# Memory keys and values as one 512-column product, a bfloat16 mask product and transposed token factors in a kernel of two transformer blocks

## Chip, cores and metric

The kernel runs on one core of a Trainium2 chip. The metric is the device time of one execution in microseconds (us), the median of several runs.

## The reference, cut to what matters

Two transformer blocks run one after the other over 256 tokens of width 1024. The first has two layers (a gated linear recurrence, HGRN2, then a latent attention, MLA), each with an attention to a memory of 256 tokens beside it and a convolutional feed-forward layer behind it. The second has a feed-forward layer, a mixer of a convolution and gated linear attention, another feed-forward layer and a gated output. All of it is float32. What the change touches:

```python
def memory_attention(qm, mem_n, w_mem_kv, qn_g, kn_g):
    kv = mem_n @ w_mem_kv                       # (256, 1024) @ (1024, 512)
    q = rms_norm(qm.reshape(B, S, MEM_HEADS, MEM_HDIM), qn_g)
    k = rms_norm(kv[..., :MEM_W].reshape(B, M, MEM_HEADS, MEM_HDIM), kn_g)
    v = kv[..., MEM_W:].reshape(B, M, MEM_HEADS, MEM_HDIM)
    s = jnp.einsum('bshd,bmhd->bhsm', q, k) * (MEM_HDIM ** -0.5)
    p = jax.nn.softmax(s, axis=-1)
    ...
# causal_block_attention (MLA, 6 heads)
    s = jnp.where(kpos[None, :] <= qpos[:, None], s, -jnp.inf)
# in front of every feed-forward layer and of the second block's mixer
    y = xf * lax.rsqrt(jnp.mean(xf * xf, axis=-1, keepdims=True) + EPS)
# in the convolution module of the second block: a LayerNorm, with one factor for each token
```

## The kernel before, in words

**Weights as a stream.** All large weights lie in one DRAM tensor `stream` of units, 128 partitions x 3072 floats (1.5 MB) each. SyncE loads unit u into slot u % 3 of `raw`; its order and its waits are written by hand (lines 343 to 387): unit u is asked for as soon as VectorE has split unit u - 3. ScalarE rounds each third (a "piece", 1024 columns) of a unit to float32r (`w_hi`, helper `copy`, line 1162; `split`, line 1180), VectorE subtracts it from the raw weight (`w_lo`, line 1743). Each engine's program is one fixed list, so a wait holds up all that stands behind it on that engine.

**Products.** A float32 product is made of three float32r matmuls (`three`, lines 418 to 420): high x high, high x low and low x high parts. `rows` (line 425) makes one with the tokens as stationary operand and the weight's columns moving, for 2 token tiles and 8 contraction tiles, so 48 matmuls; `cols` makes one with the weight as stationary operand and 256 tokens moving. `full` (line 423) is a plain matmul of any type; on float32 operands the profile records two matmuls for each.

**The start.** TensorE works through six units in this order (lines 727 to 761): the forget gates U_F and U_F + 1 (and, between them, the transposed memory), the memory's keys and values of layer 0, U_MEM0 and U_MEM0 + 1, and the queries U_Q and U_Q + 1. U_MEM0 holds 384 of the 512 columns, made in PSUM banks 0 and 1; U_MEM0 + 1 holds the other 128, made in banks 2 and 3. ScalarE evacuates a unit's banks right behind the product (`unit`, line 1184), and from the third unit on TensorE waits for the evacuation of the unit two back. For the memory product the normed memory must be there as high and low part (`y_hi` by ScalarE, `y_lo` by VectorE, line 1999, semaphore `memT_lo_done`). VectorE then norms the keys (`mem_keys`, line 1923).

**The recurrence.** Eight levels of small matmuls on float32 (`level`) alternate with rows-products: U_I, U_I + 1, U_MEM1 (384 of layer 1's memory columns, banks 4 and 5), U_MEM1 + 1 (the other 128, and 256 columns of layer 0's memory queries, banks 6 and 7), then U_G into banks 4 and 5 and U_G + 1.

**The causal mask** is added to the scores of MLA by a matmul of identity x mask, both float32, 256 columns wide, as the first of each head's accumulation (`head_S`, line 901). Around it TensorE transposes the head's queries and keys (`head_T`, line 898), ScalarE copies them, VectorE takes the maxima (line 2280), ScalarE the exponentials, VectorE scales them (lines 2289 to 2292), TensorE transposes them (`head_P`, line 924), VectorE copies that (line 2298), and `head_O` multiplies with the values. VectorE's list is: maxima of head 0, the key group 2 (from line 2258, it waits for ScalarE's query sums), maxima of head 1, scaling of head 0, maxima of head 2, copy of head 0, and so on.

**The tokens' factors.** A norm's factor for each token stands as a column [128 tokens, 1]; `spread` (line 527) makes it a row that is the same on all partitions: matmul with the column broadcast to 128x128 as stationary operand and the identity moving, twice, for four feed-forward layers and the second mixer; a sixth such place is in the LayerNorm (behind U_OUT2's fourth contraction tile).

Of the kernel before, what the change touches and what calls it, by code (L numbers as in the profile page):

```python
# [133 lines left out]
def build(nc, stream, vectors, masks, x_in, mem_in, pos_in, ple_in, fin_in, out):  # L134
    with ExitStack() as ctx:
# [193 lines left out]
        PLAIN = [0, 1, 2, 3, 4, 5] + HG_UNITS + [U_MLA, U_MLA + 1, U_MLA + 2, U_UQ, U_UQ + 1, U_UKV] + \  # L329
# [13 lines left out]
        def _(sp):  # L343
            i0 = _cols["ident"][0]
            for t in range(T):
# [12 lines left out]
            sp.dma_start(raw[:, 2, :], stream[2]).then_inc(rings[2], 16)  # L358
# [31 lines left out]
        def _(pool):  # L390
            pool.memset(zero[:, :], 0.0).then_inc(sem("zero_set"), 1)

            pool.wait_ge(sem("memT_lo_done"), 2)
            pool.memset(A(4608, HEADS * S), 0.0).then_inc(sem("r_zero"), 1)
# [9 lines left out]
            m.then_inc(sem("gA_clear"), 1)  # L404
# [7 lines left out]
        def _(pe):  # L412
# [310 lines left out]
            pe.wait_ge(sem("zero_set"), 1)  # L723
# [4 lines left out]
            for n, u in enumerate((U_F, U_F + 1, U_MEM0, U_MEM0 + 1, U_Q, U_Q + 1)):  # L728
                if n >= 2:
                    pe.wait_ge(s_evac, EV[u - 2])  # L730
                if u == U_MEM0:
                    pe.wait_ge(sem("memT_lo_done"), 1)
                    m = rows(u, 0, 384, (0, 1), y_hi, y_lo)
                elif u == U_MEM0 + 1:
                    m = rows(u, 0, P, (2, 3), y_hi, y_lo)
# [1937 lines left out]
```

## Time and profile before

| | us |
|---|---|
| median of 3 runs | 1179.88 |
| lowest and highest run | 1179.79 and 1180.44 |
| span of the profiled execution | 1179.2 |
| TensorE busy in it | 1167.9 (99%) |
| VectorE busy | 934.7 (79%) |
| ScalarE busy | 730.9 (62%) |

The profiled execution's own device time isn't listed apart from its span; the span is 0.7 us under the median. In the timelines below a row gives the start of a group in us from the span's start, then its length, then engine, line, operation, operands and count. A matmul's length contains its latency, and matmuls overlap: what one costs TensorE is the distance from its start to the next one's start. In brackets stands the idle time before it and what ended that.

### The profile page before, as it was taken

Reading aid. Unit: us, or ns where it says so; the run is one execution under the profiler, and the core shown is the slowest. Engines: PE = TensorE matmul, PEld = TensorE weight load, DVE = VectorE, ACT = ScalarE, POOL = GpSimd, SP = SyncE. Lnnn points to the kernel's source line nnn. Section 1 sums busy time; section 2 is a strip of 40 time slices with the busy share of each in tenths; the row PEclk is TensorE's granted clock in tenths of the full one; section 3 lists DMA queues with packets and bytes.
Section 4 is the critical chain, followed back from the end, with each engine's and each line's share of the span. In section 5 each row is a group of like instructions: output and inputs, shape, how many; then the busy total and the mean of one; then the engine's idle time right before and its main releaser. Section 6 shows DMA issues by size and latency. Waiting matters only on the chain.

```text
span 1179.2 us, 19449 instructions
## 1 busy us (share of the span) xinstructions
PE 1167.9 (99%) x7030; PEld 1038.7 (88%) x7030; DVE 934.7 (79%) x1831; ACT 730.9 (62%) x1353; POOL 4.1 (0%) x11
## 2 busy tenths in 40 slices
PE   9999999999999999999999999999999999999997
PEld 7999979888899888988889988888999898888886
DVE  6988878998878878998887866665799777666666
ACT  5883657666656876766665655544667665555555
POOL 0000000000000000000000000000000000000000
PEclk9999999999999999999999999999999999999999
DMA  8545253545455514555555564545454146454540
GB/s 333 215 155 190 80 197 136 216 184 208 165 215 176 199 55 161 214 215 178 195 183 198 208 214 172 202 176 198 161 184 192 49 158 249 168 205 171 203 161 36
DMA packets 21316, 211.64 MB, mean 179 GB/s; under 512 B 2625, under 2 KB 2881, under 8 KB 4481
## 3 DMA queue, kind: packets, MB, share of 16 engines
q1 hardware_dynamic: 20880, 208.90, 48.6%
q0 software_dynamic: 368, 1.84, 0.5%
q8 instruction: 43, 0.70, 0.2%
q14 instruction: 25, 0.20, 0.0%
HBM read 209.68 MB, written 1.05 MB: 179 GB/s over the span
## 4 chain that ended last, share of the span: by engine, by line
PE 93%; DVE 4%; ACT 2%; DMA 1%; issue 1%; SPq 0%; DVEq 0%; ACTq 0%
PE ps L423 39%; PE ps L418 18%; PE ps L419 17%; PE ps L420 17%; PE ps L523 1%; DVE w_lo L1743 1%; DMA x<-in_x 1%; PE ps L898 0%; ACT w_hi L1162 0%; ACT arena L1162 0%; PE ps L698 0%; DVE arena L2145 0%; DVE h_both L1825 0%; ACT L1719 0%; ACT L1652 0%
## 5 line engine op out<-in xcount | busy, mean ns | idle before, releaser
L1743 DVE TENSOR_TENSOR w_lo<-raw,w_hi 128x1024 fp32r<-128x1024 f32 (+1 forms) x390 | 448.2, 1166 | 25.7 <-ACT w_hi L1162 25.6
L1162 ACT ACTIVATE w_hi<-raw 128x1024 fp32r<-128x1024 f32 (+1 forms) x390 | 383.4, 1010 | 30.2 <-PE ps L420 26.0
L423 PE MATMUL ps<-h_both,w_hi 128*128 128x512 f32 x1088 | 386.9, 398 | 0.0
L423 PE MATMUL ps<-h_both,w_lo 128*128 128x256 f32 x1088 | 305.7, 281 | 0.0
L423 PEld LDWEIGHTS ps<-h_both,w_hi 128*128 128x128 f32 x1088 | 204.8, 188 | 49.7
L418 PE MATMUL ps<-w_hi,y_hi 128*128 128x512 f32 (+2 forms) x550 | 211.7, 385 | 0.9 <-DVE y_lo L2195 0.8
L419 PE MATMUL ps<-w_lo,y_hi 128*128 128x512 f32 (+2 forms) x550 | 208.9, 380 | 0.0
L420 PE MATMUL ps<-w_hi,y_lo 128*128 128x512 f32 (+2 forms) x550 | 208.1, 378 | 0.0
L423 PEld LDWEIGHTS ps<-h_both,w_lo 128*128 128x128 f32 x1088 | 205.7, 189 | 2.6
L1162 ACT ACTIVATE arena<-ps 128x256 f32<-128x256 f32 (+2 forms) x166 | 57.7, 396 | 151.8 <-PE ps L423 148.3
L418 PE MATMUL ps<-h_both,w_hi 128*128 128x256 f32 x520 | 148.6, 286 | 0.0
L419 PE MATMUL ps<-h_both,w_hi 128*128 128x256 f32 x520 | 147.3, 283 | 0.0
L420 PE MATMUL ps<-h_both,w_lo 128*128 128x256 f32 x520 | 147.3, 283 | 0.0
L1846 DVE TENSOR_TENSOR arena<-ps,arena 128x256 f32<-128x256 f32 x136 | 51.3, 419 | 101.6 <-ACT arena L1162 101.6
L418 PEld LDWEIGHTS ps<-w_hi,y_hi 128*128 128x128 f32 x550 | 103.5, 188 | 21.6 <-issue 2.0
L420 PEld LDWEIGHTS ps<-w_hi,y_lo 128*128 128x128 f32 x550 | 103.5, 188 | 19.2
L419 PEld LDWEIGHTS ps<-w_lo,y_hi 128*128 128x128 f32 x550 | 103.6, 188 | 14.6
L419 PEld LDWEIGHTS ps<-h_both,w_hi 128*128 128x128 f32 x520 | 99.8, 192 | 0.5
L418 PEld LDWEIGHTS ps<-h_both,w_hi 128*128 128x128 f32 x520 | 99.8, 192 | 0.5
L420 PEld LDWEIGHTS ps<-h_both,w_lo 128*128 128x128 f32 x520 | 99.8, 192 | 0.0
L1262 ACT ACTIVATE arena<-arena,vec 128x256 f32<-128x256 f32 x88 | 48.2, 595 | 79.1 <-DVE arena L1851 44.3
L1868 DVE SCALAR_TENSOR_TENSOR arena<-arena,vec 128x254 f32<-128x254 f32 (+1 forms) x176 | 77.2, 480 | 22.6 <-ACT arena L1262 22.3
(288 smaller groups left out, 1319.9 us busy)
## 6 DMA issues: line engine op xcount, KB each, us to landing
raw<-in_stream SPq DMA_DIRECT2D x129, 1536.0 KB, 6.6
raw<-in_stream SPq DMA_DIRECT2D x3, 512.0 KB, 8.3
x<-in_x SPq DMA_DIRECT2D x2, 512.0 KB, 5.4
arena<-in_mem SPq DMA_DIRECT2D x1, 1024.0 KB, 14.1
x<-in_x POOLq DMA_DIRECT2D x1, 1024.0 KB, 5.1
out<-arena SPq DMA_DIRECT2D x4, 256.0 KB, 2.1
vec<-in_vectors SPq DMA_DIRECT2D x1, 633.0 KB, 8.4
arena<-in_final POOLq DMA_DIRECT2D x1, 512.0 KB, 4.8
```

The source lines that it names most:

```text
L418: pe.matmul(o, lh, rh, start=start, stop=False, skip_group_check=True)
L419: pe.matmul(o, lh, rl, start=False, stop=False, skip_group_check=True)
L420: return pe.matmul(o, ll, rh, start=False, stop=stop, skip_group_check=True)
L423: return pe.matmul(o, l, r, start=start, stop=stop, skip_group_check=True)
L523: m = pe.transpose(xt(i, k)[:, t * P:(t + 1) * P], x[:, t, k * P:(k + 1) * P], ident)
L1162: return act.activation(o, i, ACT.Copy, scale=scale)
L1262: act.activation(cv[:, g, z * S:(z + 1) * S], tu[:, g, z * S:(z + 1) * S], ACT.Identity, scale=w(4 * z + 2), bias=w(4 * z + 3)).then_inc(s ...
L1743: dve.tensor_tensor(w_lo[:, s, a], raw[:, s, a], w_hi[:, s, a], ALU.subtract).then_inc(s_lo, 1)
L1846: dve.tensor_tensor(tu[:, g, z * S:(z + 1) * S], ps[:, half_bank(j, z), 0:S], second(i)[:, g, z * S:(z + 1) * S], ALU.add).then_inc(sem("h ...
L1868: m = dve.scalar_tensor_tensor(c, tu[:, g, z * S:(z + 1) * S - d], w, c, ALU.mult, ALU.add)
```

## The change

Three parts. (1) The 512 columns of a layer's memory product are made in two banks by one product: the load of U_MEM0 (and of U_MEM1) now gathers contraction tiles 0 to 5 with all 512 columns from two units of the same DRAM tensor, in two DMAs, one of 384-column runs (1536 B) and one of 128-column runs (512 B); the next unit gathers tiles 6 and 7. U_MEM0 + 1 has one piece to split instead of three. In layer 1 the memory queries' 256 columns fill the rest of U_MEM1 + 1, with a third DMA. The evacuation of layer 0 comes after both units, that of layer 1 too; the queries change banks. SyncE's loads of the first 12 units are written out instead of partly looped. (2) GpSimd copies identity and mask to bfloat16 once, and the mask product uses those. (3) The six spreads are PE transposes. GpSimd's semaphores become one counter.

```diff
+MEM_UNITS = {U_MEM0: 1, U_MEM0 + 1: 1, U_MEM1: 1, U_MEM1 + 1: 2}
-        used = {U_UQ: 3 * 768, R_UQ1: 3 * 384, ...
+        used = {U_MEM0 + 1: PIECE, U_UQ: 3 * 768, R_UQ1: 3 * 384, ...
...
+        Q_BANK, OWN_BANK = {1: 2, 4: 2, 5: 0}, (2, 3, 0)
-        PLAIN = [0, 1, 2, 3, 4, 5] + HG_UNITS + ...
+        PLAIN = [0, 1, 3, 4, 5] + HG_UNITS + ...
...
+            def memory_unit(u):
+                v = U_MEM0 if u < U_MEM1 else U_MEM1
+                ks = slice(0, 6) if u == v else slice(6, KT)
+                n, ring = 2 * MEM_W * (ks.stop - ks.start), rings[u % SLOTS]
+                to = raw[:, u % SLOTS, 0:n].rearrange("p (k n) -> p k n", n=2 * MEM_W)
+                a, b = (stream[v + i].rearrange("p (k n) -> p k n", n=NC3) for i in range(2))
+                sp.dma_start(to[:, :, 0:NC3], a[:, ks, :]).then_inc(ring, 16)
+                sp.dma_start(to[:, :, NC3:2 * MEM_W], b[:, ks, 0:P]).then_inc(ring, 16)
+                if u == U_MEM1 + 1:
+                    to = raw[:, u % SLOTS, n:UNIT].rearrange("p (k n) -> p k n", n=MEM_W)
+                    sp.dma_start(to, b[:, :, P:NC3]).then_inc(ring, 16)
...
-            sp.dma_start(raw[:, 2, :], stream[2]).then_inc(rings[2], 16)
+            memory_unit(U_MEM0)
...
-            at = 1
+            for u in range(SLOTS, U_OUT0):
+                one(u)
+            at = U_OUT0 // SLOTS
...
+            pool.wait_ge(sem("ident_loaded"), 16)
+            pool.wait_ge(sem("vec_loaded"), 16 * 2)
+            pool.tensor_copy(mask_b[:, 0, :], ident)
+            pool.tensor_copy(mask_b[:, 1, :], causal).then_inc(sem("pool_done"), 1)
...
+            def mem_rows(l, part, banks):
+                u = (U_MEM0, U_MEM1)[l] + part
+                for k in ((0, 1, 2, 3, 4, 5), (6, 7))[part]:
+                    a = (k - 6 * part) * 2 * MEM_W
+                    pe.wait_ge(s_lo, pieces(u, a + 2 * MEM_W))
+                    for t in range(T):
+                        tt, r = slice(t * P, (t + 1) * P), slice(a, a + 2 * MEM_W)
+                        m = three(ps[:, banks[t], :], y_hi[:, k, tt], y_lo[:, k, tt],
+                                  w_hi[:, u % SLOTS, r], w_lo[:, u % SLOTS, r], k == 0, k == KT - 1)
+                return m
...
-                    m = full(ps[:, 7, t * P:(t + 1) * P], NORM[:, t:t + 1].to_broadcast([P, P]), ident)
+                    m = pe.transpose(ps[:, 7, t * P:(t + 1) * P], NORM[:, t:t + 1].to_broadcast([P, P]), ident)
...
-                if n >= 2:
-                    pe.wait_ge(s_evac, EV[u - 2])
                 if u == U_MEM0:
+                    pe.wait_ge(s_evac, EV[U_F])
                     pe.wait_ge(sem("memT_lo_done"), 1)
-                    m = rows(u, 0, 384, (0, 1), y_hi, y_lo)
+                    m = mem_rows(0, 0, (0, 1))
                 elif u == U_MEM0 + 1:
-                    m = rows(u, 0, P, (2, 3), y_hi, y_lo)
+                    m = mem_rows(0, 1, (0, 1))
...
                 else:
+                    if n >= 2:
+                        pe.wait_ge(s_evac, EV[(U_F + 1, U_MEM0 + 1)[u - U_Q]])
...
-                    m = rows(u, 0, 384, b, y_hi, y_lo)
+                    m = mem_rows(1, 0, (4, 5))
                 else:
-                    rows(u, 0, P, b, y_hi, y_lo)
-                    m = rows(u, P, MEM_W, b, h_hi, h_lo, col=P)
+                    mem_rows(1, 1, (4, 5))
+                    m = rows(u, PIECE, MEM_W, b, h_hi, h_lo, width=MEM_W)
...
-                full(bank[:, 0:2 * P].rearrange("p (a b) -> p a b", b=P), ident,
-                     causal.unsqueeze(1).to_broadcast([P, 2, P]), True, False)
+                if h == 0:
+                    pe.wait_ge(sem("pool_done"), 3)
+                full(bank[:, 0:2 * P].rearrange("p (a b) -> p a b", b=P), mask_b[:, 0, :],
+                     mask_b[:, 1, :].unsqueeze(1).to_broadcast([P, 2, P]), True, False)
...
-            unit(U_MEM0, *[lambda t=t: copy(mk_tok[0][:, t, :], ps[:, t, 0:256]) for t in range(T)],
-                 *[lambda t=t: copy(mem_v[:, 0, t, 0:P], ps[:, t, 256:384]) for t in range(T)])
+            split(U_MEM0 + 2)
+            def memory(l, banks):
+                act.wait_ge(s_used, (U_MEM0, U_MEM1)[l] + 2)
+                for t in range(T):
+                    copy(mk_tok[l][:, t, :], ps[:, banks[t], 0:MEM_W])
+                for t in range(T):
+                    m = copy(mem_v[:, l, t, :], ps[:, banks[t], MEM_W:2 * MEM_W])
+                evac.inc(m)
...
-            unit(U_MEM0 + 1, *[lambda t=t: copy(mem_v[:, 0, t, P:256], ps[:, 2 + t, 0:P]) for t in range(T)])
+            split(U_MEM0 + 3)
+            memory(0, (0, 1))
...
                 elif u == U_MEM1:
-                    unit(u, *tok(mk_tok[1], b, 256), *tok(mem_v[:, 1], b, P, 0, 256))
+                    split(u + 2)
                 elif u == U_MEM1 + 1:
-                    unit(u, *tok(mem_v[:, 1], b, P, P), *tok(qm0, b, MEM_W, 0, P))
+                    split(u + 2)
+                    memory(1, (4, 5))
+                    evac_only(u, *tok(qm0, b, MEM_W))
...
-                dve.wait_ge(s_evac, EV[(U_MEM0, U_MEM1)[l]])
+                dve.wait_ge(s_evac, EV[(U_MEM0 + 1, U_MEM1)[l]])
```

## Rows read from the trace of the kernel before

**Rows 1.** The page, part 1: busy us, share of the span, instructions.

```profile
PE 1167.9 (99%) x7030; PEld 1038.7 (88%) x7030; DVE 934.7 (79%) x1831; ACT 730.9 (62%) x1353; POOL 4.1 (0%) x11
```

**Rows 2.** TensorE's longest wait of six: us in total, times, longest.

```profile
PE ps L423 <- POOL zero L391: 1.0, 1, 1.0
```

**Rows 3.** Timeline of TensorE: layer 0's memory product, and what follows.

```profile
36.74 0.34 PE L418 MATMUL ps<-w_hi,y_hi 128*128 128x384 f32 x1
...
45.07 0.22 PE L418 MATMUL ps<-w_hi,y_hi 128*128 128x128 f32 x1
...
50.38 0.33 PE L418 MATMUL ps<-h_both,w_hi 128*128 128x256 f32 x1
```

**Rows 4.** Timeline of TensorE: layer 1's memory product, with a level between.

```profile
95.41 0.42 PE L418 MATMUL ps<-w_hi,y_hi 128*128 128x384 f32 x1
...
103.81 0.33 PE L423 MATMUL ps<-arena 128*128 128x64 f32 x2
...
106.41 0.31 PE L418 MATMUL ps<-w_hi,y_hi 128*128 128x128 f32 x1
...
111.80 0.34 PE L418 MATMUL ps<-w_hi,h_both 128*128 128x256 f32 x1
```

**Rows 5.** Timeline of TensorE: 36 matmuls of 512 columns, then 16 transposes.

```profile
155.34 0.50 PE L418 MATMUL ps<-w_hi,y_hi 128*128 128x512 f32 x1
...
163.64 0.27 PE L698 MATMUL ps<-vec,arena 128*128 128x128 f32 x1
...
165.30 0.48 PE L418 MATMUL ps<-w_hi,y_hi 128*128 128x512 f32 x1
```

**Rows 6.** Timeline of TensorE: a spread (two products, four records) and what follows.

```profile
186.41 0.69 PE L423 MATMUL ps<-vec,small 128*128 128x128 f32 x4
186.86 0.36 PE L418 MATMUL ps<-h_both,w_hi 128*128 128x256 f32 x1
```

**Rows 7.** Timeline of TensorE in MLA: head 0's mask and P, head 1's O.

```profile
411.49 0.60 PE L423 MATMUL ps<-vec 128*128 128x256 f32 x2
411.93 1.69 PE L423 MATMUL ps<-arena 128*128 128x128 f32 x12
...
419.71 0.52 PE L924 MATMUL ps<-vec,arena 128*128 128x128 f32 x3
...
424.79 0.92 PE L423 MATMUL ps<-mem_v,arena 128*128 128x256 f32 x4
```

**Rows 8.** Timeline of VectorE: key group 2, head 0's scaling, head 1's copy.

```profile
414.68 0.36 DVE L2258 TENSOR_SCALAR small<-small 128x2 f32<-128x2 f32 x2
...
419.21 0.35 DVE L2292 TENSOR_SCALAR arena<-arena,small 128x256 f32<-128x256 f32 x1
...
424.18 0.55 DVE L2298 COPY mem_v<-ps 128x384 f32<-128x384 f32 x1
```

**Rows 9.** Line 358, the load of U_MEM0, issued at 8.0 us.

```profile
DMA to landing us min/median/max: 16.8/16.8/16.8
```

**Rows 10.** Windows: us, busy (instructions) by engine, clock, DMA share, GB/s.

```profile
24.00:26.00 2.00, 2.00 (x19) 1.89 (x18) 1.96 (x5) 2.00 (x4) 0.00 (x0) 1.00 1.06 448
163.60:165.30 1.70, 1.70 (x17) 1.66 (x16) 1.43 (x9) 0.00 (x0) 0.00 (x0) 1.00 0.00 0
```

**Rows 11.** DMA issues by size, KB each, median us to landing.

```profile
vec<-in_vectors SPq DMA_DIRECT2D x1, 64.0 KB, 3.9
```

**Rows 12.** Timeline of ScalarE: splits of U_F + 1 and of U_MEM0.

```profile
22.10 5.77 ACT L1162 ACTIVATE w_hi<-raw 128x1024 fp32r<-128x1024 f32 x6
```

**Rows 13.** Timeline of VectorE: memory's low part, splits of units 3 and 4.

```profile
32.44 3.27 DVE L1999 SCALAR_TENSOR_TENSOR y_lo<-arena,vec,y_hi 128x256 fp32r<-128x256 f32 x8
...
37.66 3.49 DVE L1743 TENSOR_TENSOR w_lo<-raw,w_hi 128x1024 fp32r<-128x1024 f32 x3
...
46.86 3.49 DVE L1743 TENSOR_TENSOR w_lo<-raw,w_hi 128x1024 fp32r<-128x1024 f32 x3
```

**Rows 14.** Timeline of ScalarE: evacuation of the memory queries, two copies.

```profile
118.13 0.67 ACT L1162 ACTIVATE x<-ps 128x256 f32<-128x256 f32 x2
```

More of the change, by code:

```diff
@@ L106, in extent @@
     else:
-        used = {U_UQ: 3 * 768, R_UQ1: 3 * 384, U_OUT0 + 2: 2 * D, U_OUT1 + 2: 2 * D, U_OUT2: 2 * D,
+        used = {U_MEM0 + 1: PIECE, U_UQ: 3 * 768, R_UQ1: 3 * 384, U_OUT0 + 2: 2 * D, U_OUT1 + 2: 2 * D, U_OUT2: 2 * D,
                 U_PROJ: 2 * D, U_GATE + 2: 2 * D}.get(u, UNIT)
@@ L159, in build @@
         zero = sb("zero", [P, P], BF16)
+        mask_b = sb("mask_b", [P, 2, P], BF16)
         trig = sb("trig", [P, 2, T, HALF])
@@ L327, in build @@
         PE_TAPS = [(3, tap) for tap in range(TAPS)] + [(2, tap) for tap in range(SHARED)]
-        PLAIN = [0, 1, 2, 3, 4, 5] + HG_UNITS + [U_MLA, U_MLA + 1, U_MLA + 2, U_UQ, U_UQ + 1, U_UKV] + \
+        PLAIN = [0, 1, 3, 4, 5] + HG_UNITS + [U_MLA, U_MLA + 1, U_MLA + 2, U_UQ, U_UQ + 1, U_UKV] + \
                 [U_IN2, U_IN2 + 1, U_IN2 + 2, U_IN2 + 3, U_IN2 + 5, U_IN2 + 6, U_PROJ]
@@ L370, in one @@
                 sp.wait_ge(s_lo, (u - SLOTS) * 3 + 3)
+                if u in MEM_UNITS:
+                    memory_unit(u)
+                    return
                 sp.dma_start(raw[:, u % SLOTS, :], stream[SWAPPED.get(u, u)]).then_inc(rings[u % SLOTS], 16)
-            at = 1
+            for u in range(SLOTS, U_OUT0):
+                one(u)
+            at = U_OUT0 // SLOTS
             for a, b in ((U_UQ // SLOTS, U_UKV // SLOTS + 1), (U_OUT2 // SLOTS, (U_OUT2 + 2) // SLOTS + 1)):
@@ L390, in _ @@
         def _(pool):
-            pool.memset(zero[:, :], 0.0).then_inc(sem("zero_set"), 1)
+            pool.memset(zero[:, :], 0.0).then_inc(sem("pool_done"), 1)
             pool.wait_ge(sem("memT_lo_done"), 2)
-            pool.memset(A(4608, HEADS * S), 0.0).then_inc(sem("r_zero"), 1)
+            pool.memset(A(4608, HEADS * S), 0.0).then_inc(sem("pool_done"), 1)
+            pool.wait_ge(sem("ident_loaded"), 16)
+            pool.wait_ge(sem("vec_loaded"), 16 * 2)
+            pool.tensor_copy(mask_b[:, 0, :], ident)
+            pool.tensor_copy(mask_b[:, 1, :], causal).then_inc(sem("pool_done"), 1)
             pool.wait_ge(sem("hg_o_ready"), T + 1)
@@ L403, in _ @@
                 m = pool.memset(gA[par][CHUNK:P, :, 0:CHUNK], 0.0)
-            m.then_inc(sem("gA_clear"), 1)
+            m.then_inc(sem("pool_done"), 1)
             pool.wait_ge(sem("late_factors"), LATE.index(6) + 1)
@@ L721, in beside_memory @@
                 pe.wait_ge(sem("y_ready"), k + 1)
-            pe.wait_ge(sem("zero_set"), 1)
+            pe.wait_ge(sem("pool_done"), 1)
             warm(34)
@@ L765, in own @@
                     n, tt = h * T + t, slice(t * P, (t + 1) * P)
-                    m = full(ps[:, n // 4, (n % 4) * P:(n % 4 + 1) * P], hk[:, h, tt], hq[:, h, tt])
+                    m = full(ps[:, OWN_BANK[n // 4], (n % 4) * P:(n % 4 + 1) * P], hk[:, h, tt], hq[:, h, tt])
                     if n % 4 == 3:
@@ L1114, in gla_y @@
                     for t in range(T):
-                        m = full(ps[:, 5, t * P:(t + 1) * P], LN[:, t:t + 1].to_broadcast([P, P]), ident)
+                        m = pe.transpose(ps[:, 5, t * P:(t + 1) * P], LN[:, t:t + 1].to_broadcast([P, P]), ident)
                     m.then_inc(sem("ln_ready"), 1)
@@ L1172, in hi @@
                 elif p == 0:
-                    n = u // SLOTS + (s > 0)
+                    n = u // SLOTS + (s > 0) + sum(e for v, e in MEM_UNITS.items() if v <= u and v % SLOTS == s)
                     act.wait_ge(rings[s], 16 * n if r is None else r * 16 + 16 * n)
@@ L1377, in queries @@
                 evac_only(U_Q + n,
-                          lambda: act.activation(hq[:, h:h + 2, :].rearrange("p a b -> p (a b)"), ps[:, 2 * n, :], ACT.Silu),
-                          lambda: act.activation(hq[:, h + 2, :], ps[:, 2 * n + 1, 0:S], ACT.Silu))
+                          lambda: act.activation(hq[:, h:h + 2, :].rearrange("p a b -> p (a b)"), ps[:, 2 - 2 * n, :], ACT.Silu),
+                          lambda: act.activation(hq[:, h + 2, :], ps[:, 3 - 2 * n, 0:S], ACT.Silu))
             split(U_Q + 2)
@@ L1393, in exps @@
                         act.wait_ge(sem("ln_done"), half + 1)
-                        act.wait_ge(sem("r_zero"), 1)
+                        act.wait_ge(sem("pool_done"), 2)
                     act.activation(right(hE[:, hh, :], m), right(hD[:, hh, :], m), ACT.Exp)
@@ L1637, in _ @@
             act.wait_ge(sem("g_s_ready"), 1)
-            act.wait_ge(sem("gA_clear"), 1)
+            act.wait_ge(sem("pool_done"), 4)
             for par in range(2):
```

4 lines of the change are left out of this document (2 added, 2 removed).

## The prediction

> **What bounds the kernel now.** I read the page's busy shares first: TensorE is busy 1167.9 us of 1179.2, VectorE 79%, ScalarE 62% [rows 1]. Then TensorE's waits: there are six, and the longest is 1.0 us [rows 2]. So nearly every microsecond is a TensorE slot, and a slot saved is time saved, as long as what TensorE asks for next is ready that much earlier. The question for each edit is thus double: how many slots go, and how early the next operand was. For slots I take the timeline, distance from one start to a later start, since a matmul's printed length overlaps the next one. For readiness I compare the end of the producer on ScalarE or VectorE with TensorE's start. All durations come from one profiled execution with a span of 1179.2 us; the median of the runs is 1179.88, and what lies around the span isn't listed, so I subtract the sum from the median and take the surroundings as unchanged. A difference of 0.2%, 2.4 us, is about what a measurement of this kernel can tell from none.
>
> **Part 1, the memory product.** Layer 0 now: 48 matmuls of 384 columns take 45.07 - 36.74 = 8.33 us (0.174 each), and 48 of 128 columns take 50.38 - 45.07 = 5.31 us (0.111 each) [rows 3]. A third of the columns costs two thirds of the time: the narrow ones are paid by the matmul, not by the column. Layer 1: 103.81 - 95.41 = 8.40 and 111.80 - 106.41 = 5.39 [rows 4]. The change makes 48 matmuls of 512 columns instead of 96. Their price stands in the trace: 36 take 163.64 - 155.34 = 8.30 us, 0.231 each with a slow first one [rows 5]; 48 come to 11.0 us. Gain in layer 0: 13.64 - 11.0 = 2.6 us; in layer 1: 13.79 - 11.0 = 2.8 us. Together **5.4 us** of slots. The memory queries' 48 matmuls keep their width.
>
> Is what follows ready? Five places:
>
> (a) The load of U_MEM0 now is 768 runs of 1536 B and 768 of 512 B, where it was 128 long rows. It landed at 8.0 + 16.8 = 24.8 us [rows 9], behind a queue that was full: DMA share 1.06, 448 GB/s [rows 10]. ScalarE began to split it at 22.10 + 3 x 0.96 = 25.0 [rows 12], so it has only 0.2 us in hand. Behind that split come ScalarE's evacuation, the memory's high part, and VectorE's low part, which ended at 32.44 + 3.27 = 35.7 [rows 13]; TensorE began the product at 36.74 [rows 3]. So a landing up to 0.2 + 1.0 = 1.2 us later costs nothing. No row shows a large load in short runs. By bytes alone nothing changes: 1.5 MB at 448 GB/s are 3.5 us either way, and earlier than that is excluded, since the bytes are the same. The upper end is the 64 KB load, 8 runs of 512 B for each of 16 engines, which took 3.9 us [rows 11], at most 0.49 us a run; but most of that is the way to the first byte and back, paid once. I take the end by bytes plus half a microsecond or so, since in a full queue nothing is paid once per run that isn't hidden behind other engines' work; that costs TensorE nothing.
>
> The Trainium skill, DMA: Bandwidth & Descriptors, section "Bandwidth" (Measured), speaks against short runs: it gives a floor of about 10.5 ns a packet. An estimate by it: 96 instead of 8 runs for each engine are 88 x 10.5 ns = 0.9 us later, within the 1.2 us in hand, so the sum would stay the same; no row here shows it.
>
> (b) TensorE reaches U_Q 2.6 us earlier, at 47.7. VectorE's list is full from the memory's low part on, so it must get shorter. It does: U_MEM0 + 1 is one piece instead of three, 3.49 us before [rows 13], two of three pieces go, 2.3 us less 0.3 for two stubs of 2 columns, so 2.0. The split of U_Q's first piece then ends at 46.86 + 1.2 - 2.0 = 46.1 [rows 13], 1.6 us ahead; its other pieces are asked for no faster than they come.
>
> (c) The evacuation of layer 0 comes later in the list, but the queries now go to banks 2 and 3, free since U_F + 1, so nobody waits for it but the key norm, and the keys' transposes stand behind the whole of U_Q.
>
> (d) In layer 1 the new wait is U_G for banks 4 and 5. In front of it TensorE has a level, 106.41 - 103.81 = 2.6 us [rows 4]. ScalarE must copy four times 256 columns, two of which take 0.67 us [rows 14]: 1.3 us and 0.2 to start, so 1.1 us in hand. Queued behind these copies are the exponentials of level 5, some 0.5 us later; VectorE's products for that level were ahead of TensorE by over 1 us, as no wait in this stretch shows.
>
> (e) SyncE's list is unrolled in the same order; two or three DMAs in place of one for U_MEM1 are issued long before they are split. GpSimd's two copies stand behind its clearing of the recurrence's tile and before the reload of x, which comes only when the recurrence is done; the mask is needed at 411.49 [rows 7].
>
> **Part 2, the mask.** A float32 mask product costs 411.93 - 411.49 = 0.44 us [rows 7]. In bfloat16 it is one matmul of 256 columns; its price lies between the 0.11 of 128 columns [rows 3] and the 0.23 of 512 [rows 5], I take 0.12. Six heads: 6 x 0.32 = 1.9 us of slots. But here readiness fails. TensorE's P of head 0 starts at 419.71 [rows 7], and VectorE's scaling that it needs ends at 419.21 + 0.35 = 419.56 [rows 8]. That comes from a VectorE list that has been full since key group 2 at 414.68 [rows 8], which waits for ScalarE's sums of a product that precedes the first mask. So the three masks before P of head 0 give back their 1.0 us there: TensorE will wait. The same for head 1's O: the copy ends at 424.18 + 0.55 = 424.73 [rows 8] and TensorE starts at 424.79 [rows 7], so the fourth mask is lost too. Behind it VectorE has idle time and follows TensorE; of the last two masks I count one and a bit. **0.4 us** of 1.9.
>
> **Part 3, the spreads.** Two float32 products are four records, 186.86 - 186.41 = 0.45 us [rows 6]. Sixteen transposes take 165.30 - 163.64 = 1.66 us [rows 5], so two take 0.2. Six spreads: 6 x 0.22 = **1.3 us**; bounds 1.0 and 1.5. What follows a spread is a product whose weights are ready, and the receivers get their factors earlier, not later.
>
> The Trainium skill, TensorE: Matmul & The Clock Gate, "Part 4: PE-mode transpose", says transposes don't count as busy for the clock. By it, trading products for transposes could only cost. Here 16 transposes in a row ran at a granted clock of 1.00 (2.4 GHz) [rows 10], after a stretch of full work; two in a row are less of a gap, so I give the rule no share in the sum.
>
> **The sum.** 5.4 + 0.4 + 1.3 = 7.1 us: 1179.88 - 7.1 = **1172.8 us**.
>
> **The rivals.**
>
> Mask whole. If VectorE's list in MLA moves up after all, all six masks count: 5.4 + 1.9 + 1.3 = 8.6, 1171.3 us. For it: the slots are there. Against: rows 7 and 8 leave 0.15 and 0.06 us. Chance 0.13.
>
> Late landing. U_MEM0 comes 2.2 to 5.2 us later, TensorE waits 1 to 4 us in front of the memory product: 1174 to 1177 us. For it: the chain of (a) has 1.2 us in hand and an unknown price. Chance 0.14.
>
> Full lists at the start. ScalarE and VectorE are so dense until 65 us that a new order costs one of them a microsecond; half of layer 0's gain goes: 1174.1. Against: both lose two pieces. Chance 0.09.
>
> Slower: run cost. The mechanism is the same queue as in (a), but priced by the run. To end slower than before by 0.2% the load must come 7.1 + 2.4 + 1.2 = 10.7 us later. With 96 runs for each engine that is (3.5 + 10.7) / 96 = 148 ns a run; from there on it decides. At 200 ns the load takes 19.2 us, 15.7 later, TensorE waits 14.5, and the time is 1187.3. Rows 11 don't exclude it (490 ns at most), but a full queue at 448 GB/s makes it unlikely. Chance 0.04.
>
> No effect. The wide product saves slots, but TensorE waits as long somewhere later, a stage being timed by something that doesn't move (a transfer, or VectorE in the recurrence): 1179 to 1180. Against: TensorE has almost no wait anywhere [rows 2], so no stage is now timed by others except the stretch in MLA. Chance 0.05.
>
> My own case has 0.55.
>
> **The numbers.** The likeliest case gives 1172.8. The range takes in the mask whole and the bounds of the wide product (10.9 to 11.1 us) below, and most of the late landing above: 1170.9 to 1175.8. Faster by over 0.2% (under 1177.5): 0.55 + 0.13 + 0.09 + 0.12 of the late landing = 0.89; within 0.2%: 0.05 + 0.02 = 0.07; slower 0.04.
>
> **What would show it.** Right: 48 matmuls of 512 columns in about 11 us twice, none of 128 with `y_hi`; the same product starting near 36.7; U_Q near 47.7 with no wait; a new wait of about 1 us of TensorE in front of P of head 0 (line 924), released by VectorE; transposes of `small`, 12 in all. Wrong: a wait of TensorE on `y_lo` of line 1999 (the landing), on ScalarE in front of U_G (the banks), or no wait at line 924 (then the mask counts whole). The whole forecast falls if 512 columns cost more than 0.28 us each there.

## The result and the profile after

The kernel after takes 1172.63 us (median of 5 runs, 1171.99 to 1173.66), the kernel before beside it 1179.88 (1179.75 to 1180.44): ratio 0.9937, 95% interval 0.9925 to 0.9949, so between 6.0 and 8.8 us faster. The forecast was 1172.8. The span of the profiled execution fell from 1179.2 to 1170.3 us, 8.9; how these two numbers go together comes below.

The page after, part 1 (busy us, share, instructions), answers to [rows 1]:

```profile
PE 1158.6 (99%) x6916; PEld 1025.4 (88%) x6916; DVE 932.4 (80%) x1831; ACT 728.5 (62%) x1349; POOL 6.4 (1%) x13
```

TensorE has 114 matmuls fewer: 96 in the memory products, 6 masks that are one record instead of two, 6 spreads with two records instead of four. It is still 99% busy, but its list of waits is no longer the one of [rows 2]. After (us in total, times, longest):

```profile
PE ps L966 <- DVE arena L2344: 1.4, 2, 1.0
PE ps L450 <- POOL zero L413: 1.0, 1, 1.0
PE ps L445 <- DVE y_lo L2247: 0.8, 1, 0.8
PE ps L903 <- DVE arena L2197: 0.7, 1, 0.7
PE ps L562 <- DVE h_both L1877: 0.5, 1, 0.5
PE ps L450 <- DVE mem_v L2350: 0.3, 1, 0.3
PE ps L450 <- ACT arena L1704: 0.3, 1, 0.3
```

L966 is `head_P`: two new waits behind VectorE's scaling. `L450 <- DVE mem_v` is new too, `head_O` behind VectorE's copy. The rest was there; of the six waits before, the 0.7 us in front of the first norm is gone.

The timeline of TensorE, layer 0's memory product (to [rows 3]), then layer 1's (to [rows 4]):

```profile
35.95 0.47 PE L445 MATMUL ps<-w_hi,y_hi 128*128 128x512 f32 x1
...
46.95 0.28 PE L445 MATMUL ps<-h_both,w_hi 128*128 128x256 f32 x1
...
91.93 0.47 PE L445 MATMUL ps<-w_hi,y_hi 128*128 128x512 f32 x1
...
100.22 2.79 PE L450 MATMUL ps<-arena 128*128 128x64 f32 x24
102.81 0.48 PE L445 MATMUL ps<-w_hi,y_hi 128*128 128x512 f32 x1
...
105.66 0.28 PE L445 MATMUL ps<-w_hi,h_both 128*128 128x256 f32 x1
```

Layer 0: 46.95 - 35.95 = 11.00 us where 13.64 stood. Layer 1's first six tiles take 100.22 - 91.93 = 8.29; then comes a level, and the last two tiles take 105.66 - 102.81 = 2.85. Together 11.14, where 13.79 stood. U_Q has no wait in front of it.

The spread of the first feed-forward layer (to [rows 6]) costs 180.39 - 180.22 = 0.17 us where it was 0.45, and the granted clock around it is 1.00 (window: us, busy and instructions by engine, clock, DMA share, GB/s):

```profile
180.22 0.41 PE L570 MATMUL ps<-vec,small 128*128 128x128 f32 x2
180.39 0.36 PE L445 MATMUL ps<-h_both,w_hi 128*128 128x256 f32 x1
```

```profile
180.20:180.60 0.40, 0.40 (x7) 0.40 (x6) 0.40 (x1) 0.05 (x1) 0.00 (x0) 1.00 0.00 0
```

MLA in TensorE's timeline (to [rows 7]): a mask product costs 405.20 - 405.09 = 0.11 us, and three places wait (in brackets):

```profile
405.09 0.27 PE L450 MATMUL ps<-mask_b 128*128 128x256 bf16 x1
405.20 1.70 PE L450 MATMUL ps<-arena 128*128 128x128 f32 x12
...
413.31 0.52 PE L966 MATMUL ps<-vec,arena 128*128 128x128 f32 x3 [0.96 <-DVE arena L2344]
...
418.12 0.92 PE L450 MATMUL ps<-mem_v,arena 128*128 128x256 f32 x4 [0.32 <-DVE mem_v L2350]
...
425.17 0.55 PE L966 MATMUL ps<-vec,arena 128*128 128x128 f32 x3 [0.40 <-DVE arena L2344]
```

They are P of head 0, O of head 1 and P of head 4. Before, TensorE stood about 0.1 us at each of the three, too short for its list of waits.

**Where the 8.9 us of the span are.** I cut TensorE's timeline at four starts: the first norm's transposes, the memory product, `head_T(0)` in MLA, and U_OUT1's product behind MLA. An ordinary table, each length a difference of two starts (the last one: span minus start):

| us | before | after | difference |
|---|---|---|---|
| span's start to norm | 12.09 | 11.19 | 0.90 |
| norm to memory product | 24.65 | 24.76 | -0.11 |
| memory product to T of head 0 | 369.59 | 363.98 | 5.61 |
| MLA, T of head 0 to U_OUT1 | 26.79 | 26.20 | 0.59 |
| U_OUT1 to the span's end | 746.08 | 744.17 | 1.91 |

Part 1 and one spread are in the third line, part 2 in the fourth, five spreads in the fifth. Two things in it are no slot of the change. The first line is when `x` and its first statistics came: over the 14 profiled executions of this study the norm started anywhere from 10.45 to 12.26 us, whatever the kernel. In these two profiles the second load of `x` landed at 8.4 us before and at 7.5 after. And 0.6 of the last line lies behind the last operation of VectorE; an experiment below is about it. From the norm on the difference is 8.00 us, without the 0.6 it is 7.4.

The second line hides a loss: `e2_mask_alone` and `e3_spreads_alone` below, which leave this stretch as it was before, took 24.48 us in it, so 24.76 is 0.28 us more and not 0.11.

The device time also has a part outside the span. Device time minus span, taken execution by execution (spans are listed to 0.1 us), was 1.74 to 1.83 us in 48 executions of the kernel before (timed beside the experiments; the medians of their spans were 1178.0 to 1178.5 us on the four chips) and 1.99 to 3.06 us, median 2.52, in the five of the kernel after (median span 1170.3). So some 0.7 us of what the span lost came back outside it, which is why the medians differ by 7.25 us only. What that part is and why it grew, no run here shows.

### The profile page after: what moved, and what is told of

Same layout as the page of the kernel before. It is cut to its first block, busy times and chain, and to the rows that moved or that the text cites. A ratio compares the mean times of both kernels' runs of the same rounds, so it can differ in the third digit from the quotient of the medians.

```text
span 1170.3 us, 19211 instructions
## 1 busy us (share of the span) xinstructions
PE 1158.6 (99%) x6916; PEld 1025.4 (88%) x6916; DVE 932.4 (80%) x1831; ACT 728.5 (62%) x1349; POOL 6.4 (1%) x13
## 4 chain that ended last, share of the span: by engine, by line
PE 94%; DVE 4%; ACT 2%; issue 0%; POOL 0%; DVEq 0%; ACTq 0%; POOLq 0%
PE ps L450 39%; PE ps L445 18%; PE ps L446 17%; PE ps L447 17%; PE ps L562 1%; DVE w_lo L1795 1%; ACT arena L1204 0%; PE ps L737 0%; DVE arena L2197 0%; ACT w_hi L1204 0%; PE ps L938 0%; DVE arena L2322 0%; DVE h_both L1877 0%; DVE small L2333 0%; PE ps L570 0%
## 5 line engine op out<-in xcount | busy, mean ns | idle before, releaser
L450 PE MATMUL ps<-h_both,w_hi 128*128 128x512 f32 x1088 | 386.8, 398 | 0.0
L450 PE MATMUL ps<-h_both,w_lo 128*128 128x256 f32 x1088 | 305.4, 281 | 0.0
L450 PEld LDWEIGHTS ps<-h_both,w_hi 128*128 128x128 f32 x1088 | 204.4, 188 | 50.0
L450 PEld LDWEIGHTS ps<-h_both,w_lo 128*128 128x128 f32 x1088 | 205.4, 189 | 2.6
L445 PE MATMUL ps<-w_hi,y_hi 128*128 128x512 f32 (+1 forms) x518 | 204.6, 395 | 1.0 <-DVE y_lo L2247 0.8
L446 PE MATMUL ps<-w_lo,y_hi 128*128 128x512 f32 (+1 forms) x518 | 201.7, 389 | 0.0
L447 PE MATMUL ps<-w_hi,y_lo 128*128 128x512 f32 (+1 forms) x518 | 201.0, 388 | 0.0
L445 PEld LDWEIGHTS ps<-w_hi,y_hi 128*128 128x128 f32 x518 | 97.3, 188 | 23.2 <-issue 2.2
L447 PEld LDWEIGHTS ps<-w_hi,y_lo 128*128 128x128 f32 x518 | 97.3, 188 | 20.5
L446 PEld LDWEIGHTS ps<-w_lo,y_hi 128*128 128x128 f32 x518 | 97.4, 188 | 15.8
```

The lines of the kernel that those rows point to most:

```text
L445: pe.matmul(o, lh, rh, start=start, stop=False, skip_group_check=True)
L446: pe.matmul(o, lh, rl, start=False, stop=False, skip_group_check=True)
L447: return pe.matmul(o, ll, rh, start=False, stop=stop, skip_group_check=True)
L450: return pe.matmul(o, l, r, start=start, stop=stop, skip_group_check=True)
```

## The experiments

Each was timed in 5 rounds against the kernel before on the same chip (5 executions; 11 of e2 and e3, 4 of e11). The start of an execution scatters by about 1 us, and so do single executions of one kernel. For changes under 1 us I therefore read the lengths of the table above. Where nothing in them was changed, MLA repeats to 0.1 us and the stretch before it to 0.2 us (363.81 to 364.00 in after, e5, e6, e7, e9 and e12).

**The parts one by one.** `e1_memory_alone` is the kernel after with float32 mask and spreads, without GpSimd's copies:

```diff
-  full(bank[:, 0:2 * P].rearrange(...), mask_b[:, 0, :], mask_b[:, 1, :].unsqueeze(1).to_broadcast([P, 2, P]), True, False)
+  full(bank[:, 0:2 * P].rearrange(...), ident, causal.unsqueeze(1).to_broadcast([P, 2, P]), True, False)
-  m = pe.transpose(ps[:, 7, t * P:(t + 1) * P], NORM[:, t:t + 1].to_broadcast([P, P]), ident)
+  m = full(ps[:, 7, t * P:(t + 1) * P], NORM[:, t:t + 1].to_broadcast([P, P]), ident)
```

> Part 1 alone: the mask product and the spreads are those of before. Theory: two products save 2.64 and 2.65 us of slots (as in the profile after), about 0.3 us is given back in front of the memory product: 1179.9 - 5.0 = 1174.9 us, and the product takes 11.0 us in each layer. Rival, more is lost to the new order of ScalarE's and VectorE's lists: 1176 or more. Rival, part 1 carries nearly the whole gain of 7.25 us: 1173 or less.

Measured 1174.7 us beside 1180.25 (0.9953, 0.9940 to 0.9967): 5.5 us. The memory product to T of head 0 takes 364.07 us, 5.52 less than before; 5.29 of it are the two products, the rest is about what this length scatters by. VectorE's last operation ends 3.1 us before the span's end, where it was 3.7: the 0.6 at the end is there without any of the spreads. `e2_mask_alone` and `e3_spreads_alone` are the kernel before with the other halves of the same lines.

> Part 2 alone: the kernel before with the bfloat16 mask product. Theory: 6 x 0.33 = 2.0 us of slots go, but about 1.0 us comes back as a wait of TensorE in front of P of head 0 and 0.3 in front of O of head 1: 1179.9 - 0.6 = 1179.3 us, with both waits, released by VectorE. Rival, the mask whole: 1177.9 us, without these waits.

Measured 1179.58 us (0.9995, 0.9986 to 1.0004), which alone can't be told from no change; MLA takes 26.20 us instead of 26.79. TensorE's waits in MLA are those of the kernel after, in total, times and longest:

```profile
PE ps L932 <- DVE arena L2300: 1.4, 2, 1.0
...
PE ps L429 <- DVE mem_v L2306: 0.3, 1, 0.3
```

So the loss belongs to the mask alone, not to its meeting with the other parts.

> Part 3 alone: the kernel before with six transposed spreads. Theory: 6 x 0.27 = 1.6 us: 1178.3 us, granted clock 1.00 behind each spread. Rival, a pair of transposes lets TensorE's clock fall or its receivers wait: 1179.9 us or more.

Measured 1178.52 us (0.9986, 0.9977 to 0.9995): 1.7 us by the medians. By the lengths 369.59 - 369.35 = 0.24 for the first spread, and 746.08 - 745.04 = 1.04 for the other five, to which 0.28 has to be added: this execution's last store ended 4.0 us behind VectorE's last operation, where it was 3.72 before. Together 1.56 us. The three parts add up: 5.5 + 0.7 + 1.7 = 7.9 by the medians, within what they scatter of 7.25.

**Is it the readiness of P of head 0?** `e5_mask3_f32` puts the float32 mask back for heads 0 to 2 only.

```diff
+  if h < 3:
+      full(bank[:, 0:2 * P].rearrange(...), ident, causal.unsqueeze(1).to_broadcast([P, 2, P]), True, False)
+  else:
       full(bank[:, 0:2 * P].rearrange(...), mask_b[:, 0, :], ...)
```

> The kernel after, with the float32 mask product again for heads 0 to 2 alone. Theory: these three add 3 x 0.33 = 1.0 us of slots, and the 0.96 us wait in front of P of head 0 shrinks to under 0.1: no change, 1172.6 us. Rival, the wait has another cause and stays: 1173.6 us.

Measured 1172.6 us (0.9938, 0.9925 to 0.9952): no change. TensorE's timeline of this kernel:

```profile
411.27 0.60 PE L450 MATMUL ps<-vec 128*128 128x256 f32 x2
411.70 1.69 PE L450 MATMUL ps<-arena 128*128 128x128 f32 x12
413.50 0.52 PE L970 MATMUL ps<-vec,arena 128*128 128x128 f32 x3
...
418.58 0.92 PE L450 MATMUL ps<-mem_v,arena 128*128 128x256 f32 x4 [0.49 <-DVE mem_v L2354]
```

P of head 0 has no wait left, and 1.0 us of mask slots came back in its place: counted from T of head 0 it starts at the same time as after, 13.4 us. MLA as a whole took 26.48 us, 0.28 more than after, and all of it is there by O of head 1 (18.47 us behind T of head 0, 18.19 after, 18.46 before). So of the 1.0 us of the first three masks 0.7 is worth nothing and 0.3 is had, at O of head 1.

`e6_vector_order` then moves the list instead of the mask.

```diff
 (key group 2, behind its reciprocal square roots)
+    head_S(1)
+    head_P(0)
 (VectorE's list)
     k_group(2)
-    head_S(1)
-    head_P(0)
     head_S(2)
     head_pT(0)
     head_P(1)
-    lo(None, U_OUT1, 0)
     head_P(2)
     head_S(3)
     head_pT(1)
     head_pT(2)
+    lo(None, U_OUT1, 0)
     head_P(3)
 (ScalarE's list)
-    hi(None, U_OUT1, 0)
     head_E(1)
+    hi(None, U_OUT1, 0)
```

> The kernel after, with VectorE's list in MLA changed: head 1's maxima and head 0's scaling go ahead of the scaling inside key group 2, the split of U_OUT1's first piece goes behind the copy of head 2, and on ScalarE head 1's exponentials go ahead of that piece. Theory: P of head 0 no longer waits 0.96 us; head 4's transposes (key group 2) or head 3's scores then wait 0.3 to 0.5 us: gain 0.5 to 0.8 us, about 1172.0. Rival, all of the 1.3 us of waits are had: 1171.3. Rival, the list is full however it is ordered, and the whole wait moves to head 4's transposes: 1172.6.

Measured 1172.04 us (0.9933, 0.9919 to 0.9947). TensorE's timeline:

```profile
412.05 0.55 PE L966 MATMUL ps<-vec,arena 128*128 128x128 f32 x3
412.98 1.10 PE L938 MATMUL ps<-vec,arena 128*128 128x128 f32 x8 [0.38 <-DVE small L2328]
...
424.41 0.55 PE L966 MATMUL ps<-vec,arena 128*128 128x128 f32 x3 [0.67 <-DVE arena L2346]
```

MLA takes 25.68 us, 0.52 less than after. P of head 0 comes at once, key group 2 is now 0.38 late for head 4's transposes, and the wait at P of head 4 grew from 0.40 to 0.67. `e9_list_two` treats that one:

```diff
+    head_S(4)
-    lo(None, U_OUT1, 1)
     for i in range(5, HEADS + 3):
-        if i <= HEADS: head_S(i - 1)
         if i <= HEADS + 1: head_pT(i - 2)
-        if i == 5: lo(None, U_OUT1, 2)
+        if i <= HEADS: lo(None, U_OUT1, i - 4)
         if i <= HEADS: head_P(i - 1)
         y_lo_from(...)
+        if i == 5: head_S(5)
```

> The kernel with the changed VectorE list, and two more moves there: head 4's maxima go ahead of U_OUT1's second piece, and head 5's maxima and the third piece go behind head 4's scaling. Theory: TensorE stood 0.67 us in front of P of head 4 behind these two splits (1.2 us each on VectorE); the wait falls under 0.1: 1172.0 - 0.6 = 1171.4 us. The 0.38 us in front of head 4's transposes stays. Rival, the wait only moves to P of head 5 or to the output product's pieces: 1172.0.

Measured 1172.25 us (0.9930, 0.9917 to 0.9944), MLA 25.43 us: 0.25 less than e6, where 0.6 was expected, since 0.40 us of wait stays. VectorE's timeline of `e12_long_first` (below), which has the same list, shows why:

```profile
420.92 0.29 DVE L2337 TENSOR_REDUCE small<-ps 128x1 f32<-128x128 f32 x1 [0.77 <-PE ps L453]
...
422.13 1.22 DVE L1798 TENSOR_TENSOR w_lo<-raw,w_hi 128x1024 fp32r<-128x1024 f32 x1
423.26 0.16 DVE L2346 RECIPROCAL small<-small 128x2 f32<-128x2 f32 x1
```

The second piece's split now stands between the copy and head 4's scaling, whose exponentials were done by 422.9, and VectorE sat idle 0.77 us ahead of the maxima, where the split had fitted. My own reordering put it in the wrong gap. The median does not resolve a change of this size, and the norm of its profiled execution started at 12.26 us, 1.07 later than that of the kernel after.

**Short runs.** In the kernel after, SyncE's list looks like this (SPq is its queue, the second number how long it stood at the instruction):

```profile
7.49 0.44 SPq L356 DMA_DIRECT2D raw<-in_stream  x1
7.97 5.17 SPq L357 DMA_DIRECT2D raw<-in_stream  x1
13.18 4.91 SPq L376 DMA_DIRECT2D arena<-in_masks  x1
18.13 0.44 SPq L356 DMA_DIRECT2D raw<-in_stream  x1
```

Before, the issues of U_MEM0's load and of the masks took 0.45 and 0.44 us. ScalarE's timeline shows when the load was there, and VectorE's when the memory's low part, for which TensorE's product waits, was done (32.58 + 3.26 = 35.84; the product starts at 35.95):

```profile
25.07 2.96 ACT L1204 ACTIVATE w_hi<-raw 128x1024 fp32r<-128x1024 f32 x3 [1.31 <-DMA raw<-in_stream]
...
32.58 3.26 DVE L2051 SCALAR_TENSOR_TENSOR y_lo<-arena,vec,y_hi 128x256 fp32r<-128x256 f32 x8 [1.45 <-ACT y_hi L1204]
```

`e4_long_rows` changes how the host lays out the weights: the units of the memory products lie in DRAM as they are loaded, so one DMA of 128 rows each.

```diff
-  u = [..., model(mk[0], 0, 384), model(mk[0], 384, 512)]
+  u = [..., unit(grid(mk[0])[:, 0:6]), unit(grid(mk[0])[:, 6:8])]
-  u += [model(mk[1], 0, 384), model(mk[1], 384, 512, hg, 3072, 3328)]
+  u += [unit(grid(mk[1])[:, 0:6]), unit(grid(mk[1])[:, 6:8], grid(hg[:, 3072:3328]))]
```

> The kernel after, but the memory's units lie in DRAM as they are loaded (128 rows of 12 KB each), so U_MEM0 is one DMA again. Theory: the landing at 25.1 us is what TensorE waits for at the memory product; it comes about 1 us earlier, and with it the product by 0.3 us: 1172.6 - 0.3 = 1172.3 us, SyncE free by about 8.5 us. Rival, the short runs cost nothing that decides: 1172.6. Rival, they cost ScalarE's and VectorE's lists more, up to the whole 1 us: 1171.6.

Measured 1172.62 us (0.9940, 0.9927 to 0.9954). SyncE and ScalarE:

```profile
7.55 0.49 SPq L351 DMA_DIRECT2D raw<-in_stream  x1
8.08 0.44 SPq L367 DMA_DIRECT2D arena<-in_masks  x1
16.41 0.33 SPq L351 DMA_DIRECT2D raw<-in_stream  x1
```

```profile
24.45 2.95 ACT L1195 ACTIVATE w_hi<-raw 128x1024 fp32r<-128x1024 f32 x3 [0.55 <-DMA raw<-in_stream]
```

From issue to ScalarE's start: 24.45 - 7.55 = 16.90 us, and 25.07 - 7.49 = 17.58 with the short runs, so 0.7 later in this pair. Over all profiles, U_MEM0 landed 15.9 to 16.9 us behind its first issue in the six with long rows there (median 16.65) and 16.9 to 18.1 us in the seven with these short runs (median 17.5): 0.9 us later, or 10 ns for each of the 88 added runs an engine. Norm to memory product takes 24.49 us instead of 24.76: the 0.27 expected is there. The median gained nothing; 0.6 us came back at the very end (below).

`e7_short_runs` goes the other way, the 384-column runs as three DMAs of 128-column runs:

```diff
-  sp.dma_start(to[:, :, 0:NC3], a[:, ks, :]).then_inc(ring, 16)
+  for j in range(3 if u == U_MEM0 else 1):
+      c = slice(j * P, (j + 1) * P) if u == U_MEM0 else slice(0, NC3)
+      sp.dma_start(to[:, :, c], a[:, ks, c]).then_inc(ring, 16)
```

> The kernel after, with all of U_MEM0's load in runs of 512 B: four DMAs of 768 runs each in place of one of 768 runs of 1536 B and one of 768 runs of 512 B. Theory, a small price for each run inside a full queue: the first 1408 added runs (88 an engine) made the landing about 0.6 us later, so 96 more an engine make it 0.65 us later still, and now all of it reaches TensorE: 1173.2 us. Rival, the issue decides (SyncE stood 5.2 us at the second DMA): each further DMA comes 5 us later, landing about 10 us later, TensorE waits about 10 us: 1183 us. Rival, the runs cost nothing: 1172.6.

Measured 1173.15 us (0.9947, 0.9933 to 0.9960). ScalarE's split with VectorE's low part, TensorE's product, and SyncE:

```profile
25.77 2.96 ACT L1206 ACTIVATE w_hi<-raw 128x1024 fp32r<-128x1024 f32 x3 [2.91 <-DMA raw<-in_stream]
...
33.29 3.26 DVE L2053 SCALAR_TENSOR_TENSOR y_lo<-arena,vec,y_hi 128x256 fp32r<-128x256 f32 x8 [2.86 <-ACT y_hi L1206]
```

```profile
36.65 0.47 PE L447 MATMUL ps<-w_hi,y_hi 128*128 128x512 f32 x1 [1.11 <-issue]
```

```profile
6.50 9.78 SPq L358 DMA_DIRECT2D raw<-in_stream  x3
16.33 2.77 SPq L359 DMA_DIRECT2D raw<-in_stream  x1
```

From issue to split it is 25.77 - 6.50 = 19.27 us: 1.7 more than after, for 96 more runs an engine. But the first issue came 1.0 us earlier here than in the kernel after, so the load may only have stood longer behind the others: e6, with the short runs of after and issued nearly as early (6.75), took 18.1 us. Against it the step is 1.1 us. So it is 12 to 18 ns a run, and one profile can't tell that from the 10 ns of the first step. The product starts right behind the low part, which ends at 33.29 + 3.26 = 36.55. Norm to memory product is 25.68 us, 0.9 more than after. SyncE stood 9.8 us at the first three of the four DMAs and 2.8 at the last, but the transfers went on meanwhile: the rival of 10 us is out, and with it any price near the 148 ns a run from which the change would have lost.

**What a matmul's width costs.** `e8_two_halves` and `e11_four_quarters` cut each 512-column matmul of both memory products into two of 256, or four of 128:

```diff
-  m = three(ps[:, banks[t], :], y_hi[:, k, tt], y_lo[:, k, tt], w_hi[:, u % SLOTS, r], w_lo[:, u % SLOTS, r], k == 0, k == KT - 1)
+  for j in range(2):                          # 4 and P in the other
+      r = slice(a + j * MEM_W, a + (j + 1) * MEM_W)
+      m = three(ps[:, banks[t], j * MEM_W:(j + 1) * MEM_W], ..., k == 0 and j == 0, k == KT - 1)
```

> The kernel after, with each 512-column matmul of the memory products cut into two of 256 columns (96 in place of 48 for each layer). Theory: only narrow ones under 256 columns cost more than their columns, 256 cost 0.12 us as in the forget gates: 96 x 0.12 = 11.5 in place of 11.0 in each layer, 1173.6 us. Rival, a fixed cost for each matmul (on the line through 0.111 us at 128 columns and 0.174 at 384, 0.142 at 256): 13.6 us in each layer, the whole gain gone, 1177.9 us.

> The kernel after, with each 512-column matmul of the memory products cut into four of 128 columns (192 in place of 48 for each layer). Theory: a matmul of 128 columns costs 0.111 us, nearly as much as one of 256 (0.12): 192 x 0.111 = 21.3 in place of 11.0 in each layer, 1172.6 + 20.6 = 1193.2 us. Rival, the 0.111 of before came from the wait for the pieces of U_MEM0 + 1, and a narrow matmul costs by its columns (0.06): 11.5 in each layer, 1173.6 us.

Measured 1173.07 us (0.9940, 0.9927 to 0.9954) and 1193.11 us (1.0107, 1.0091 to 1.0122). Layer 0's product in the latter, TensorE's timeline:

```profile
36.05 0.22 PE L445 MATMUL ps<-w_hi,y_hi 128*128 128x128 f32 x1
...
57.44 0.33 PE L445 MATMUL ps<-h_both,w_hi 128*128 128x256 f32 x1
```

That is 21.39 us for 192, 0.111 each; the halves take 47.80 - 36.27 = 11.53 for 96, 0.120 each. So 128 columns cost 0.111, 256 cost 0.120, 384 cost 0.174 [rows 3] and 512 cost 0.229 us. From 256 on one pays by the column; below, nearly the price of 256. Every one of these matmuls has a load of its stationary operand beside it; whether that load or the matmul itself sets the lowest price was not tried.

**The end of the span, and the last kernel.** VectorE's last operation ends at 1166.45 + 0.75 = 1167.20 us after, 3.1 before the span ends, and at 1175.48 before, 3.7 before its end:

```profile
1166.45 0.75 DVE L2572 SCALAR_TENSOR_TENSOR arena<-x,small,arena 128x512 f32<-128x512 f32 x1
```

Every kernel with short-run loads has 3.1 here (8 of them up to that point), every one without has 3.6 to 4.0 (before, e2, e3, e4 and `e10_best`, which is e9's lists with the long rows).

> The two moves of VectorE's list together with the long rows for U_MEM0 and U_MEM1. Theory: the long rows are worth 0 to 0.3 us, as the landing decides only where the first rows of x came early: 1171.2 us. Rival, they add nothing: 1171.4.

It gave 1172.3 us (0.9937, 0.9924 to 0.9951): norm to product 24.49 and MLA 25.43 as hoped, and 3.67 us at the end, which takes the gain of the rows away. The last kernel has e9's lists, long rows for layer 0 and the short runs of after for layer 1:

> The kernel with both moves of VectorE's list, layer 0's memory units in long rows and layer 1's in short runs as in the kernel after. In the profiles so far the span ends 3.1 us behind VectorE's last operation wherever the memory units are loaded in short runs, and 3.6 to 4.0 us behind it where none is. Theory A, any short runs on SyncE's queue do it: 3.1 us again, and from the first norm's start to the end 1157.9 us, 1171.8 as a median. Theory B, it is U_MEM0's short runs at the start: 3.7 us and 0.6 us more. Theory C, it varies from execution to execution whatever the kernel: either value, and then it belongs to no part of the change.

Measured **1171.76 us** beside 1179.78 (0.9927, 0.9914 to 0.9941). Its VectorE ends here, in a span of 1169.2 us:

```profile
1165.35 0.75 DVE L2574 SCALAR_TENSOR_TENSOR arena<-x,small,arena 128x512 f32<-128x512 f32 x1
```

That is 3.1 us again, as theory A says. Norm to the end is 1157.92 us, where 1159.11 stands after and 1167.11 before. It has the lowest median here. Against the kernel after 0.9 us of medians from different chips is not resolved; the 1.2 us of the lengths is the better evidence, and the five spans of each do not overlap (1168.8 to 1169.8 us against 1170.0 to 1170.6).

Theory A has a rival. The profile's DMA queues in the last 3.2 us of the span (packets, MB, share of 16 engines), first of `e4_long_rows` (window 1167.30:1170.50), then of `e12_long_first` (1166.00:1169.20):

```profile
q1 hardware_dynamic: 288, 0.52, 43.7%
q14 instruction: 1, 0.01, 1.2%
...
q1 hardware_dynamic: 288, 0.52, 43.8%
```

The data are the same, but in e4 a packet of the instruction queue lies among the last stores. It is there in all five kernels with 3.6 to 4.0 us, and in none of the nine with 3.1, where the last such packet comes 16.7 us before the end. The nine also have more DMAs on SyncE's list (148 to 152 against 145). So what the nine share may be where in a list the next instructions are fetched and not the short runs as such. No run separates the two: that would be a kernel with long rows and a few more DMAs.

## Why the prediction held, step by step

**Part 1, 5.4 us forecast.** Shown: 5.5 us alone; in the kernel after 2.64 in layer 0 and 2.65 in layer 1, where I had 2.6 and 2.8. The price from [rows 5] carried over as it stood. Layer 1 is 0.1 short because its product comes in two stretches, and the first matmul of each costs 0.3 instead of 0.23 us.

**Place (a), the landing, "costs TensorE nothing".** Here a size was off. The landing came 0.9 us later, where I had taken half a microsecond because a run's price would be hidden in a full queue; it was not hidden. I had 1.2 us in hand, but that reserve was read from one execution in which the norm had started at 12.09 us. The chain of the memory goes by the load and not by the norm; where `x` comes early, TensorE is early and the reserve gone. After started its norm at 11.19 and lost 0.27; e6 at 10.45 and took 25.32 us from norm to product, 0.83 over the 24.49 of e4. With the same short runs, e11 had its norm at 11.56 and took 24.49. So the loss is 0 to 0.8 us by the execution. The late landing's rival, 1 to 4 us, did not come.

In these runs the first 88 more runs an engine made the load 0.9 us later, the next 96 another 1.1 to 1.7. The Trainium skill, DMA: Bandwidth & Descriptors, section "Bandwidth", gives 10.5 ns a packet as a floor, for loads issued by GpSimd; from it I had estimated 0.9 us for the first 88. The trace agrees with that estimate, which I had put beside the sum and not into it. The same estimate for the next 96 runs is 1.0 us, a little under what was measured.

**Places (b) to (e).** U_Q came at 46.95 us with no wait, no wait stands in front of U_G, and GpSimd's copies were in nobody's way. SyncE's list is where (e) had nothing: it gave the issue of the extra DMAs no time, and SyncE stood 5.2 and 4.9 us. What it issued behind them was not urgent: the masks went out 4.7 us later and unit 3 0.7 us later, and nobody waited.

**Part 2, 0.4 us forecast of 1.9.** Shown: 0.59 of 6 x 0.33 = 1.98. The two places named, P of head 0 and O of head 1, are where TensorE waits, 0.96 and 0.32 us, and a third is P of head 4 with 0.40. For P of head 0 e5 shows the cause: put the slots back and the wait is gone. e6 shows it from the other side. The rival "mask whole" is out. The shares within the sum were not as I had them. I gave the first four masks nothing and the last two 0.4 us. By the distances from T of head 0, O of head 1 came 0.27 us earlier, which e5 puts down to the first three masks; the fifth mask brought its whole 0.33, and the sixth nothing: what stands in front of it was already 0.58 us earlier, and P of head 4 behind it is 0.58 earlier too. That the sum came within 0.2 us is in part luck.

**Part 3, 1.3 us forecast.** Shown: 1.56 us by the lengths of e3, 1.7 by its medians, a little over my upper bound of 1.5: two transposes cost 0.17 us where I had 0.2, so a spread saves 0.26 and not 0.22. The granted clock stays at 1.00 (2.4 GHz) around them. The Trainium skill, TensorE: Matmul & The Clock Gate, "Part 4: PE-mode transpose", says that a transpose doesn't count as busy for the clock in the way that a matmul does; two in a row in the middle of full work show no cost from that here.

**The sum.** The lengths give 5.34 + 0.59 + 1.58 = 7.5 us (5.61 less the first spread's 0.27; MLA; the spreads' 0.27 and 1.91 - 0.6 for the other five), less 0.1 at the landing: 7.4, against 7.1. The 0.6 at the end was in no step of mine. Nor was the part of the device time outside the span: I took the surroundings as unchanged, and they grew by some 0.7 us. The two nearly cancel, so that the median, 7.25, lies so close to 7.1 is in part luck; that the slots gave 7.4 where 7.1 was forecast is not. The interval of the median holds all of these. The 0.9 of the span's start is chance, so of the span's 8.9 only 8.0 can belong to the change.

## What to carry to other kernels

Price a replaced instruction by the distance between starts in a stretch that already has the new shape; that held within 0.15 us for each stretch here. A slot saved counts only up to the next operand's end: compare each with the producer's list, and if the list is the limit, move its non-urgent work (here splits of 1.2 us) behind what TensorE needs next, in the same change. Reserves at the start of a kernel should be read off several executions, since the first loads don't land at the same time twice.

## What the runs showed of the hardware

- A matmul of 128 float32r columns costs 0.111 us, one of 256 0.120: widths under 256 are hardly cheaper.
- SyncE stood 5.2 us at a DMA of 768 runs of 512 B and 4.9 at the next one, for the masks; with four DMAs of 768 such runs it stood 9.8 us at the first three and 2.8 at the last. The transfers lost only 0.9 and then 1.1 to 1.7 us more, so there the engine that issues was held up much longer than the data. It is not the form of the DMA alone: the DMA of 768 runs of 1536 B just before took 0.44 us to issue, and that of 768 runs of 512 B for layer 1, at 56.4 us, 0.55.
- The span ended 3.1 us behind VectorE's last operation in all nine kernels with short-run loads on SyncE's queue, and 3.6 to 4.0 us in the five without, though these loads are over 1000 us before. The five have a packet of the instruction queue in the last 3 us and the nine have none. Which of the two decides was not tried; it is worth 0.6 us of the span.
- Device time minus span was 1.74 to 1.83 us in all 48 executions of the kernel before, and 1.99 to 3.06 us in the five of the kernel after. A saving in the span need not arrive whole in the device time.
